# The odd recurrence of a three-block network, cut into four interleaved streams

## The reference, cut to what matters

```python
q = pf[None] + mu[:, None, None, :] * (shifted - pf[None])
r, k, v, wd, ad = jnp.split(q, RWKV_SPLITS, axis=-1)
z_w = w0[:, None, None, :] + jnp.einsum('dbsl,dlc->dbsc', jnp.tanh(wd), w2)
decay = jnp.exp(-jnp.exp(-jax.nn.softplus(-z_w) - 0.5))
a = jax.nn.sigmoid(a0[:, None, None, :] + jnp.einsum('dbsl,dlc->dbsc', ad, a2))
kk = heads(k * k_k)
kk = kk * lax.rsqrt(jnp.maximum(jnp.sum(kk * kk, axis=-1, keepdims=True), 1e-12))
k = k * (1.0 + (a - 1.0) * k_a)
...
def wkv7_step(state, inp):
    r, w, k, v, a, b = inp          # w = decay, a = -kk, b = kk * a
    sa = jnp.einsum('...ij,...j->...i', state, a)
    state = (state * w[..., None, :] + sa[..., :, None] * b[..., None, :]
             + v[..., :, None] * k[..., None, :])
    y = jnp.einsum('...ij,...j->...i', state, r)
    return state, y
```

## Time and profile before

| | us |
|---|---|
| median of 3 runs (4971.11 to 4972.32) | 4971.45 |
| the profiled execution | 4975.08 |
| its span, first to last instruction | 4973.3 |
| recurrence, first products to round 13 | 3929.4 to 4686.1 |
| its rounds 14 and 15 | 4686.1 to 4780.3 |

### The profile page before, as it was taken

One profiled execution on the slowest core, in us unless ns is written; L12 is line 12 of the kernel. 1 busy time (PEld: TensorE's weight loads), 2 busy tenths in 40 slices (PEclk: granted clock), 3 DMA queues, 4 the chain that ended last, 5 costly groups with the idle time before them and its releaser, 6 DMA issues.

```text
span 4973.3 us, 64889 instructions
## 1 busy us (share of the span) xinstructions
PE 4589.2 (92%) x28316; PEld 3408.7 (69%) x28316; DVE 2548.8 (51%) x4403; ACT 845.3 (17%) x1490; POOL 123.6 (2%) x228
## 2 busy tenths in 40 slices
PE   9999998879998999799989999989999788888899
PEld 7886445557886888356656488858887666666644
DVE  5675865334545456553344265556454355555511
ACT  0001023111022000321222100011000233333210
POOL 0000000000000000000000000000000011111000
PEclk9998999868999999899999999989899888878899
DMA  6524442004222222111111222222222000000021
GB/s 238 179 94 58 65 65 51 1 1 85 93 86 67 85 91 87 36 41 51 51 43 35 68 85 85 68 85 86 67 88 77 27 2 2 2 2 2 19 96 42
DMA packets 284954, 311.69 MB, mean 63 GB/s; under 512 B 7168, under 2 KB 277632, under 8 KB 281600
## 3 DMA queue, kind: packets, MB, share of 16 engines
q1 hardware_dynamic: 284672, 307.55, 21.7%
HBM read 305.43 MB, written 2.10 MB: 62 GB/s over the span
## 4 chain that ended last, share of the span: by engine, by line
PE 49%; DVE 5%; ACT 3%; issue 1%; DMA 0%; POOL 0%; DVEq 0%; POOLq 0%; ACTq 0%; SPq 0%
PE ps L348 18%; PE ps L272 13%; PE ps L2125 1%; PE ps L317 1%; PE ps L833 1%; PE ps L471 1%; PE ps L2928 1%; PE ps L2857 1%; PE ps L849 1%; PE ps L3179 1%; PE ps L2846 1%; PE ps L2946 1%; PE ps L818 1%; PE ps L1845 1%; PE ps L2665 1%
## 5 line engine op out<-in xcount | busy, mean ns | idle before, releaser
L272 PE MATMUL ps<-main,w 128*128 128x512 f32 (+1 forms) x2832 | 1245.2, 596 | 21.9 <-DMA w<-in_ffn_wg 12.2
L348 PE MATMUL ps<-main 128*128 128x256 f32 x5136 | 1139.2, 379 | 0.0
L348 PEld LDWEIGHTS ps<-main 128*128 128x128 f32 x5136 | 975.5, 190 | 133.1
L272 PEld LDWEIGHTS ps<-main,w 128*128 128x128 f32 x2832 | 543.2, 195 | 647.3 <-issue 619.6
L348 PE MATMUL ps<-main,w 128*128 128x256 f32 x3872 | 863.9, 379 | 1.4 <-DVE main L416 1.4
L348 PEld LDWEIGHTS ps<-main,w 128*128 128x128 f32 x3872 | 736.1, 190 | 105.8 <-issue 4.3
L435 DVE TENSOR_TENSOR main<-main,ps 128x512 f32<-128x512 f32 x164 | 112.8, 688 | 417.7 <-PE ps L348 417.5
L661 DVE SCALAR_TENSOR_TENSOR main<-main,params_sb 128x512 f32<-128x512 f32 x256 | 192.5, 752 | 9.1
L387 ACT COPY main<-ps 128x256 f32<-128x256 f32 x98 | 36.5, 372 | 896.3 <-PE ps L348 896.3
L432 DVE TENSOR_TENSOR main<-main,ps 128x512 f32<-128x512 f32 x98 | 67.3, 687 | 221.6 <-PE ps L348 218.8
L440 DVE TENSOR_TENSOR main<-main,ps 128x512 f32<-128x512 f32 x164 | 112.8, 688 | 78.0 <-PE ps L348 76.7
(11 more groups left out here) (456 smaller groups left out, 4985.2 us busy)
## 6 DMA issues: line engine op xcount, KB each, us to landing
w<-in_w_in SPq DMA_DIRECT2D x58, 1024.0 KB, 7.0
w<-in_e_w_in SPq DMA_DIRECT2D x28, 1024.0 KB, 5.0
main<-in_ada_w SPq DMA_DIRECT2D x24, 1024.0 KB, 5.0
w<-in_ffn_wg SPq DMA_DIRECT2D x22, 1024.0 KB, 6.4
w<-in_ffn_wu SPq DMA_DIRECT2D x22, 1024.0 KB, 6.3
w<-in_o_w_in SPq DMA_DIRECT2D x20, 1024.0 KB, 5.5
w<-in_ffn_wd SPq DMA_DIRECT2D x16, 1024.0 KB, 5.1
w<-in_w_up SPq DMA_DIRECT2D x16, 1024.0 KB, 5.5
```

What stands on the lines that cost most here:

```text
L272: i = pe.mm(PS[b][:, 0:n], wv[:, k, f * 128:(f + 1) * 128], g.X(kg + k), start=kg + k == 0, stop=kg + k == g.nk - 1)
L348: t = pe.mm(PS[b][:, 256 * half:256 * half + 256], weight[:, m, :], x(m), start=m == 0, stop=m == n - 1)
```

## The change

`products` is split into `head` and `body`, the norm after an odd generation becomes `tail`, and rounds have these streams, each with one turn per pass: chain r, inverse r+1, body r+2, head r+3 (from the sixth pass on), and in even rounds the tail of r-1. The last tail runs by itself.

```diff
-    def rw_rounds(e, products, inverse, chain, aside):
+    def behind(turns, steps):
+        for _ in range(turns):
+            yield
+        yield from steps
+
+    def together(*streams):
+        streams = list(streams)
+        while streams:
+            streams = [g for g in streams if next(g, "end") != "end"]
+            yield
+
+    def rw_rounds(e, head, body, inverse, chain, tail, aside):
         none = iter(())
-        run(products(e, 0))
+        run(head(e, 0))
+        run(together(body(e, 0), behind(5, head(e, 1))))
         for r in range(-1, 16):
-            streams = [chain(e, r) if r >= 0 else none]
-            second = [inverse(e, r + 1) if r < 15 else none]
-            third = [products(e, r + 2) if r < 14 else aside(e, r)] * (2 if r < 15 else 1)
-            streams += third + second if e.name == "act" else second + third
-            while [g for g in streams if next(g, "end") != "end"]:
-                pass
+            ends = tail(e, r - 1) if r > 0 and r % 2 == 0 else none
+            own = behind(0, chain(e, r)) if r >= 0 else none
+            whole = inverse(e, r + 1) if r < 15 else none
+            feeds = body(e, r + 2) if r < 14 else aside(e, r)
+            ahead = behind(5, head(e, r + 3)) if r < 13 else none
+            run(together(*((own, whole, feeds, ahead, ends) if e.name == "act" else (own, whole, feeds, ahead, ends))))
+        run(tail(e, 15))
         e.fence("rwkv")
```

The head on ACT, with tanh for the sigmoids (1 + tanh(x/2) is twice a sigmoid; the factor 1/2 goes into constants `HW`, `OM` and the exponents), and on DVE:

```diff
+    def act_rw_head(a, i):
+        ...
+        a.act(t_sg, bank("rw w", i), ACT.Tanh, scale=0.5, bias=hw(8 * d + ft)).then_inc(
+            a.inc(s, "out", "rw w", i), 1)
+        a.wait_ge(*at("mm", "rw a", i))
+        a.act(t_al, bank("rw a", i), ACT.Tanh, scale=0.5, bias=hw(16 + 8 * d + ft)).then_inc(
+            a.inc(s, "out", "rw a", i), 1)
+        yield
...
         act_shifted(a, s, ("rw k", i), t_k, 8 + ft, d)
         yield
         a.wait_ge(*at("rw k", i))
         a.act(t_kk, t_k, ACT.Square, scale=par("o_k_k_3", ft)).then_inc(a.inc(s, "rw kk square", i), 1)
         yield
+        a.wait_ge(*at("rw pc", i))
+        tail = Pc[:, :, 128:129]
+        a.act(s1, s4_ if d == 0 else tail[:, :, 0], ACT.Exp, scale=-C0 / 2).then_inc(a.inc(s, "rw s1", i), 1)
+        a.act(s2, tail[:, :, 0] if d == 0 else s4_, ACT.Exp, scale=-C0 / 2).then_inc(a.inc(s, "rw s2", i), 1)
+        a.act(s3, s3, ACT.Exp, scale=-C0 / 2).then_inc(a.inc(s, "rw s3", i), 1)
+        yield
+        a.act(t_ep, Pc, ACT.Exp, scale=-C0 / 2).then_inc(a.inc(s, "rw ep", i), 1)
+        a.act(t_en, Pc, ACT.Exp, scale=C0 / 2).then_inc(a.inc(s, "rw en", i), 1)
+        yield
...
         for c in range(NT):
-            v.scan(Pc[:, c, 1:129], ones, t_sg[:, c * 128:(c + 1) * 128], 0.0, MUL, ADD).then_inc(v.inc(s, "rw scan", i), 1)
-        yield
+            v.scan(Pc[:, c, 1:129], ones, t_sg[:, c * 128:(c + 1) * 128], 0.0, ADD, ADD).then_inc(v.inc(s, "rw scan", i), 1)
+        yield
```

The body on PE; its scores, turned keys and own products stand in turns 3 to 12, and DVE picks each kind of scores in the same turn:

```diff
+    def pe_rw_body(pe, i):
+        s = sem["pe", "rwkv"]
+        FM, VK, MS = FMs[i % 3], VKs[i % 3], MSs[i % 6]
+        pe_rw_spread(pe, ("rw kk all", i), r_st[0], ("rw kk rstd", i))
+        yield
+        yield
+        yield
+        pe_rw_scores(pe, i, 0)
+        yield
+        pe_rw_turned(pe, i, 2, FM(3), ("rw f4", i))
+        yield
+        yield
+        pe_rw_scores(pe, i, 1)
+        yield
+        pe_rw_turned(pe, i, 1, FM(2), ("rw f3", i))
+        yield
+        pe_rw_scores(pe, i, 2)
+        yield
+        pe_sum(pe, ("rw bonus", i), [t_r], [("rw kr", i)], block)
+        pe_rw_turned(pe, i, 0, t_v, ("rw v", i))
+        yield
+        pe_rw_scores(pe, i, 3)
+        yield
```

The products with 64 moving columns get their 128-wide weights in two halves (L2946 and L3179), and POOL takes all four quarters of the inverse's start:

```diff
-                        t = pe.mm(PS[b][:, c * 128 + 64 * hd:c * 128 + 64 * hd + 64], MS[hd](1)[:, s_], vs,
-                                  start=True, stop=True)
+                        for h in HALF:
+                            t = pe.mm(PS[b][h, c * 128 + 64 * hd:c * 128 + 64 * hd + 64],
+                                      part128(MS[hd](1), c)[:, h], vs, start=True, stop=True)
...
-                t = pe.mm(PS[b][:, 64 * hd:64 * hd + 64], DT(hd)[:, s_], rhs[:, 64 * hd:64 * hd + 64],
-                          start=True, stop=True)
+                for h in HALF:
+                    t = pe.mm(PS[b][h, 64 * hd:64 * hd + 64], part128(DT(hd), c)[:, h], rhs[:, 64 * hd:64 * hd + 64],
+                              start=True, stop=True)
...
-            for quarter in QUARTERS[0:2]:
+            for quarter in QUARTERS:
                 start_blocks(p, s, ("rw", i), MT8[i % 2], r_d1, i % 2 == 0, [quarter])
                 p.wait_ge(*at("inv first", "pool", "rw", i))
-            p.wait_ge(*at("inv first", "dve", "rw", i))
             start_inverse(p, s, ("rw", i), r_d1)
```

More of the change, by code:

```diff
@@ new lines, in pe_rw_scores @@
+    def pe_rw_scores(pe, i, kind):
+        s, FM = sem["pe", "rwkv"], FMs[i % 3]
+        lh, rh = r_kinds[kind]
+        for f in (lh, rh):
+            pe.wait_ge(*at(f"rw f{f + 1}", i))
+        two = [banks.take("rw ms", i, 4 * hd + kind) for hd in range(2)]
+        for b, before in two:
+            if before:
+                pe.wait_ge(*at("out", *before))
+        for c in range(NT):
+            s_ = slice(c * 128, (c + 1) * 128)
+            for hd in range(2):
+                t = pe.mm(PS[two[hd][0]][:, s_], FM(lh)[H2[hd], s_], FM(rh)[H2[hd], s_], start=True, stop=True)
+                if c == NT - 1:
+                    t.then_inc(pe.inc(s, "mm", "rw ms", i, 4 * hd + kind), 1)
@@ L2901, in pe_rw_products @@
+    def pe_rw_body(pe, i):
+        s = sem["pe", "rwkv"]
+        FM, VK, MS = FMs[i % 3], VKs[i % 3], MSs[i % 6]
         pe_rw_spread(pe, ("rw kk all", i), r_st[0], ("rw kk rstd", i))
         yield
-        for _ in range(5):
-            yield
-        pe_sum(pe, ("rw bonus", i), [t_k], [("rw kr", i)], block)
         yield
         yield
[L2908 to L2924, removed]
-            for c in range(NT):
-                s_ = slice(c * 128, (c + 1) * 128)
-                for hd in range(2):
-                    t = pe.mm(PS[two[hd][0]][:, s_], FM(lh)[H2[hd], s_], FM(rh)[H2[hd], s_], start=True, stop=True)
-                    if c == NT - 1:
-                        t.then_inc(pe.inc(s, "mm", "rw ms", i, 4 * hd + kind), 1)
-            yield
-            yield
@@ L2933, in pe_rw_products @@
-        for k in range(3):
-            pe.wait_ge(*at("out", "rw tp", i, k))
+        pe_rw_scores(pe, i, 0)
[12 more added lines that the diff above has]
+        yield
@@ L2999, in act_rw_products @@
         yield
+        act_rw_turned(a, i, 2)
         yield
-        if i > 2:
-            a.wait_ge(*at("mm", "rw y", i - 3, NT - 1))
-        for k in range(3):
-            a.wait_ge(*at("mm", "rw tp", i, k))
-            a.copy(VK(k), bank("rw tp", i, k)).then_inc(a.inc(s, "out", "rw tp", i, k), 1)
-            yield
-        for k in range(8):
-            yield
+        yield
+        yield
+        act_rw_turned(a, i, 1)
+        yield
+        yield
+        act_rw_turned(a, i, 0)
+        yield
+        yield
         a.wait_ge(*at("mm", "rw rhs own", i))
```

195 lines of the change are left out of this document (99 added, 96 removed).

## The result

The changed kernel takes 4778.5 us (median of 4 runs, 4772.3 to 4782.6) against 4971.9; the ratio is 0.961 with a 95% interval of 0.9593 to 0.9627. The forecast was 4790.0. The execution that was profiled is the slowest of the four (4782.6).

The account below looks back on a forecast made before the run. Bound by a chain going from engine to engine. Rounds 0 to 13 -173.3, start -11.8, end +3.6 sum to -181.5 us: 4975.08 becomes 4793.6, less 3.6 for the median, 4790.0 us; range 4735 to 4885.

Parts of the forecast that it names:

- What bounds it, and that the idle time goes: Rounds 0 to 13: no engine fills the 48.4 us, a cross-engine chain binds; new round 36.0 us, PE work plus 4.0.
- the layout: Turn-by-turn plan of a new round at the high clock: 3.0 us of idle PE, plus 1.0 added for queue waits.
- four places: In the old round, PE stands while one other engine works alone, said to be on a generation two rounds ahead.
- The clock taken as high throughout: Rounds 0 to 13: no idle stretch long enough for a low clock; PE work falls from 40.9 to 34.0 us.
- The order of the streams: In each round, chain, inverse, body and head interleave turn by turn, dealing out lumped waits; 14.4 us a round within reach.
- The rival of hand-offs: Rounds 0 to 13: fixed-order waits keep half the idle time, a round of 42 us, 4874 in all; chance 0.19.
- The halves: 64-wide weights in pairs at L2946 and L3179 save 2.0 us of PE work a round.
- the term of L2946: Eight products of 1.93 us become 16 taking 1.08 us, saving 0.85 us a round.
- A further price for changes of tiling mode: At L3179's groups, 0.3 us for each further mode change would make the sum some 17 us higher; not counted.
- Tanh: Gates on ACT: one table load of 1.28 us a round goes, counted as nothing because mostly covered.
- POOL at no cost: POOL takes DVE's two quarters of the inverse's start; DVE loses 1.26 us a round, and the cost is nothing.
- Start and end: First products and round -1 gain 11.8 us, round 14 nothing; the last tail alone costs 3.6 us.

Follow-up runs that it names:

- tail edits: Changed kernel with DVE's reciprocal of the norm's root one turn later and the last tail beside round 15's dense products: 4769.8 us.
- The lump: Changed kernel with the DVE product that forms f3 done seven times in a row in each generation: 4883.5 us.
- a like amount of work dealt out: Changed kernel with six additional DVE instructions a generation, one at a time (f3, f2 and four picks each done twice): 4838.4 us.

## Why the prediction was right, and where it was not
*What bounds it, and that the idle time goes.* Right: 35.4 us a round for 36.0, PE busy for 32.4 for 32.0, idle for 3.0 for 4.0 (the layout gave 3.0, to which I had added 1.0). In a round without a tail the places are right too: 1.3 us for DVE at the start (1.4 laid out), 0.4 in turn 7 (1.0), 0.4 for ACT's copies at the end (0.3). The 0.3 for the gates' bank was not in the layout, which had every former user of a bank done a turn before; it comes to 1.9 us in rounds 0 to 13. One of the four places was misread: the copies at 4341.64 in the earlier trace rows (L901) are the inverse's own last ones, no work of a later generation, and they end a round of after as they did in before.

*The clock taken as high throughout.* Right for rounds 0 to 13 (0.99), and it is about half of the gain. The lump shows the mechanism: one wait of 5.85 us brought 1.2 GHz for 6.8 us and 2.0 us of PE time; a like amount of work dealt out left the clock at 1.00 in rounds without a tail (0.92 in one with). How long a wait must be for that is not told by these runs: round 14 was at the low clock in one kernel and at the high one in another with the same wait.

*The order of the streams.* The prediction explained the gain by dealing out, and named in passing that the head is wanted only a round later; the run with head and body in one round has dealt-out streams as well and is 4.2% slower than before. What the other parts are worth in after is small: 17 us for the halves, 4 at the most for tanh, some 12 for POOL. So about 160 of the 193 us are the order's. But dealing out does not carry them by itself. That the head's lead carries it is the reading that fits the waits of that run (DVE for an input that ACT has not made), but it is argued and not shown, since the edit moved other turns as well. The rival of hand-offs named the danger (one wait on DVE holds three streams) but had its price far too low: 42 us a round, where that order gives about 60.

*The mean hides two kinds of round.* 33.4 and about 38.4 us: the tail costs 5 us every second round, 4.5 of them busy time of PE, some at the low clock (0.96). The prediction had the mean round only (PE's work for the norm is in the mean of before that it started from).

*The halves.* Right in direction; the term of L2946 was right (0.85), that of L3179 too large: 4 x 0.33 was expected and 0.77 came, since the group went from 0.60 to 0.38 us and not to 0.27. As a whole 1.6 us of PE for 2.0. A further price for changes of tiling mode, which the rule from the Trainium skill (TensorEngine Tiling (Array Packing), "Key Properties") would have added, is not seen in the sum: the halves give 17 us in after and 34 in before. The 0.3 us for it in the prediction is from no row, and no run here shows it.

*Tanh.* Counted at nothing, and nothing to 4 us is what it is. There are two loads a round (L2994 and L3017, 13 of each), as the Trainium skill's table sets have it (ScalarE: Activation LUTs, "Table sets: the hidden batching unit").

*POOL at no cost.* This step failed. The prediction looked at POOL's slack alone and not at what POOL's reads do to DVE: "rw kr" +0.41 us, f3 +0.22, and smaller amounts on f2 and the shifted inputs, together about 1.0 us of DVE a round, nearly as much as the two quarters (1.26) that DVE got rid of. What it costs the round is less: in one without a tail the only wait of PE that stands behind these instructions is the 0.4 us for L3289. DVE was to have 26.7 us a round and has 26.8, but by luck. Added one by one, its instructions take 418.6 us in rounds 0 to 13 for 424.1 in before, and of that difference some 4.5 us are one head and one norm product less in the window (the scans L3068 are x52 where L3032 was x56); the rest of the fall is that successive instructions overlap more, which busy time counts once. The move looks right still: going back costs 1.2 us a round without a tail.

*Start and end.* Start -14.7 for -11.8. Round 14 was put at 0 and cost 1.8; with its clock high it would be about 28 us, a gain of 3 (tail edits). Round 15 and the rest: +5.7 for +3.6. PE's idle time at the last tail is 2.4 us, less than the 3.6 expected, since the table load runs beside the sum that the root waits for. But PE is also busy for 3.2 us more from round 15 on. The first 8 dense products are in part at the low clock (5.93 us, 3.6 to 3.7 at the high one), but so they were in before (5.40), and they explain 0.5 of it; the last tail's spread is low in part (1.68 us for 1.09), and so are the dense products behind it. The prediction counted idle time here but no clock, though it had done both for the rounds.

Summed by the spans: -189.5 us without the 3.1 that lie ahead of the stage, for -181.5 expected: -9.0 too little for the rounds, -2.9 too little for the start, and +3.9 too little for the end. Together they are 8 us, and with the 3.1 ahead of the stage the 11 by which the sum was off.

## What to carry to other kernels
When several generations share in-order engines, let every stream use what an earlier round has finished before you interleave them: interleaving head and body of one generation within a round cost more here than it gave (5181.7 us for 4971.6). Price an idle stretch of PE with the low clock behind it, by the rows at both levels: here a 5.5 us longer wait cost 7.5. Before putting an instruction on an engine that waits, look at who stands behind it, and at which reads of a neighbour engine will lie beside whose.

## What the runs showed of the hardware
DVE's products with two SBUF operands run longer while POOL's products with SBUF operands run: 1.46 us for one of 0.74, 1.22 for 0.75, and in the lump 1.10 in the median and up to 1.46 for 0.69. Beside POOL's zero fills, which read nothing, they stay at 0.69; DVE's instructions with an operand in PSUM (L930 and L939 of after) take 0.47 to 0.49 us for two with POOL's products beside them and without. One kind more is hit: the scaling of an SBUF tile by a column of SBUF (L3292 of after) takes 0.53 to 0.72 us for 0.28. POOL's own got longer too (L919 1282 ns in after, 1097 in before). The Trainium skill has this as a rule (SBUF — State Buffer, "SBUF: two separate sides"): a DVE instruction with two SBUF inputs and a GpSimd one that reads SBUF exclude each other for a whole instruction. The trace agrees for the instructions with two SBUF inputs; how the blocking is cut it does not show, only records up to about twice as long.

The granted clock fell to 0.50 within the 5.85 us wait and stayed there for 4.9 us more with PE fully busy; a like stretch, 6.1 us, stands in the earlier trace rows. A wait of 1.32 us was followed, 0.3 us on, by 10.2 us at the low clock in one kernel and by none in another. The time of a float32 product of 64 moving columns goes with the width of its weights too: halving them, at twice the number of products, takes eight from 1.93 to 1.08 us.
